# Splitting the row, memory-key and memory-value products of a decoder block into high and low parts, and spreading eight softmax steps over the stream

## The reference

```python
def hybrid_mixer(xn, ...):
    proj = xn @ w_mix_in                     # 1304 columns of q, keys, values, gates; 3 x 512 of the conv
    q, kc, vc, ks, vs, kw, vw, gl, ch, cb, cc = jnp.split(proj, splits, axis=-1)
    q, kc, ks, kw = (rope(a, positions) for a in (q, kc, ks, kw))
    o_nsa = nsa_attention(...)               # compressed keys, and two causal softmaxes, 8 heads in 2 groups
    u = cc * ch                              # conv: 3 taps along the tokens, then times cb
    o = concatenate([rmsnorm(o_nsa), rmsnorm(o_conv)])
    return o @ w_mix_out

h = h + hybrid_mixer(rmsnorm(h), ...)
h = h + memory_cross_attention(rmsnorm(h), rmsnorm(mem), w_xq, w_xkv, w_xo)   # k, v = split(memn @ w_xkv)
h = h + moe_ffn(rmsnorm(h), ...)             # router, top 4 of 32 experts, SwiGLU
return rmsnorm(h, g_final)
```

## Time and profile before

| | |
|---|---|
| time, three runs | 1242.11 us median (1241.1, 1242.11, 1246.43) |
| the profiled execution | 1248.39 us, of which the span of instructions is 1246.4 us |
| PE busy | 1147.8 us, 92% of the span |
| DVE, ACT, POOL busy | 288.1, 186.7, 74.8 us |
| HBM read | 443.6 MB, 357 GB/s over the span |
| mean granted PE clock | 0.989 of 2.4 GHz |

### The profile page before, as it was taken

The page is one execution under the profiler, slowest core; times in us unless marked ns, Lnnn a source line. Parts: engine busy times, 40 slices in busy tenths (PEclk is TensorE's granted clock), DMA queues, the critical chain, the costliest instruction groups (busy, mean ns, idle before and its releaser), DMA issues.

```text
span 1246.4 us, 12486 instructions
## 1 busy us (share of the span) xinstructions
PE 1147.8 (92%) x5441; PEld 493.1 (40%) x5442; DVE 288.1 (23%) x584; ACT 186.7 (15%) x358; POOL 74.8 (6%) x48
## 2 busy tenths in 40 slices
PE   7879988999999999999999899899999998999896
PEld 4576656565433333333333333333333333333332
DVE  3474353221421111221111111121211111111111
ACT  3220354133200000100000000010000000000001
POOL 0450043022000000000000000000000000000000
PEclk9989999999999999999999999999999999999998
DMA  8705503367899999999999999999999999999994
GB/s 339 248 3 231 172 1 135 135 226 293 367 427 427 428 427 427 427 428 427 429 427 429 426 427 428 427 427 428 428 426 428 427 427 426 429 428 427 429 427 175
DMA packets 44135, 445.47 MB, mean 357 GB/s; under 512 B 6040, under 2 KB 10224, under 8 KB 19408
## 3 DMA queue, kind: packets, MB, share of 16 engines
q1 hardware_dynamic: 41936, 444.37, 85.7%
q10 hardware_dynamic: 2144, 0.30, 0.1%
HBM read 443.60 MB, written 1.05 MB: 357 GB/s over the span
## 4 chain that ended last, share of the span: by engine, by line
PE 61%; DMA 32%; DVE 3%; ACT 3%; issue 1%; SPq 0%; DVEq 0%
DMA R<-in_w_gate_up 20%; PE ps L1572 18%; PE ps L1581 13%; DMA XMT<-in_w_gate_up 7%; PE ps L1435 4%; PE ps L1170 4%; DMA XM<-in_w_gate_up 3%; PE ps L1601 3%; PE ps L1548 3%; PE ps L1206 3%; PE ps L1270 2%; PE ps L1228 2%; PE ps L1275 2%; PE ps L1370 2%; PE ps L1563 1%; ACT A L728 1%
## 5 line engine op out<-in xcount | busy, mean ns | idle before, releaser
L1572 PE MATMUL ps<-R,convT 128*64 128x512 f32 x1232 | 274.7, 594 | 26.0 <-DMA R<-in_w_gate_up 26.0
L1097 DVE TENSOR_SCALAR A<-ps 128x512 f32<-128x512 f32 x32 | 22.1, 691 | 695.2 <-PE ps L1572 695.2
L1572 PEld LDWEIGHTS ps<-R,convT 128*64 128x64 f32 x1232 | 85.2, 137 | 203.1 <-issue 149.0
L1581 PE MATMUL ps<-R,A 128*64 128x512 f32 x608 | 134.8, 592 | 0.0
L723 ACT ACTIVATE A<-A 128x512 f32<-128x512 f32 x32 | 20.2, 630 | 508.3 <-DVE A L1097 508.3
L1581 PEld LDWEIGHTS ps<-R,A 128*64 128x64 f32 x608 | 42.7, 137 | 78.2 <-issue 76.8
L1601 PE MATMUL ps<-A,convT 64*128 64x512 f32 x256 | 63.6, 615 | 1.4 <-ACT A L730 1.4
L1548 PE MATMUL ps<-H,convT 128*64 128x512 f32 x256 | 60.4, 592 | 0.3 <-DVE convT L1052 0.3
L730 ACT COPY A<-ps 128x512 f32<-128x512 f32 x32 | 18.7, 585 | 238.4 <-PE ps L1581 238.4
L1572 PE MATMUL ps<-XMT,convT 128*64 128x512 f32 x208 | 47.0, 594 | 3.7 <-DMA XMT<-in_w_gate_up 3.7
L1572 PE MATMUL ps<-QK,convT 128*64 128x512 f32 x208 | 47.0, 594 | 2.4 <-DMA QK<-in_w_gate_up 2.3
(11 more groups left out here) (278 smaller groups left out, 1111.2 us busy)
## 6 DMA issues: line engine op xcount, KB each, us to landing
R<-in_w_gate_up SPq DMA_DIRECT2D x77, 2048.0 KB, 40.9
R<-in_w_down SPq DMA_DIRECT2D x38, 2048.0 KB, 43.3
QK<-in_w_gate_up SPq DMA_DIRECT2D x13, 2048.0 KB, 40.8
A<-in_w_gate_up SPq DMA_DIRECT2D x13, 2048.0 KB, 40.8
XMT<-in_w_gate_up SPq DMA_DIRECT2D x13, 2048.0 KB, 42.2
XM<-in_w_gate_up SPq DMA_DIRECT2D x12, 2048.0 KB, 42.4
XM<-in_w_down SPq DMA_DIRECT2D x7, 2048.0 KB, 44.7
QK<-in_w_down SPq DMA_DIRECT2D x7, 2048.0 KB, 43.3
```

The lines of the kernel that those rows point to most:

```text
L1572: last = mm(bank(b)[s * SLOTS:(s + 1) * SLOTS, :], xg[:, 4 * (j % 2) + 2 * c + j // 2, :], w[:, c * 2 * FF + at + s * BANK:c * 2 * FF + at ...
L1581: last = mm(bank(O_BANK)[s * SLOTS:(s + 1) * SLOTS, :], hTm[:, c, i * SLOTS:(i + 1) * SLOTS], w[:, c * D + s * BANK:c * D + (s + 1) * BANK ...
```

## The change

**Products.** A *unit* is one 512-column block of a weight matrix for one chunk of 128 inputs, split into a high and a low part and multiplied with both halves of the tokens: six matmuls of 512 columns (`unit(u)`, `split_mm`). There are 24 units for the conv (h, c, b, now with tokens on the partitions), 16 for the memory values and 16 for the keys. The rows use the same product (`rows(kc)`, both halves in one pass, three buffers `row_hi`, low parts on DVE). ACT writes every high part; DVE the low parts of rows and conv, POOL those of the memory units. High parts have four buffers up to unit 24 and eight (`HIB`) after.

**Norms.** x and memory are transposed as they come; the root goes in later, as a scale on the way out of PSUM (and in the sine and cosine for the rope). Since the conv and keys now come out with tokens on the partitions, u, b and the keys are transposed after (16 for the conv, 16 for the keys, `key_transposes`).

**Order.** The rope's pieces alternate with the low parts of units 4 to 19 on DVE. The 32 memory units are laid over the softmax steps by `U_AT`, ACT and POOL running `U_AHEAD` = 5 units ahead. On DVE weigh(n) comes right after mask_max(n), and its last instruction is now four `tensor_scalar` in place of one `tensor_tensor`. The hidden layer of the compressed keys uses four column groups of PE in place of two. POOL's constants for the experts wait for the second pv of the cross-attention (it was the second scores), since memory values stand where they are written.

```diff
+HIB = 8
+        ROW_AT = [(R, R_p, kc * ROWC) for kc in range(6)] + [(R, R_p, 22528), (A, A_p, ROWB * ROWC)]
+        row_hi = [QK_p[:, b * ROWC:(b + 1) * ROWC] for b in range(ROWB)]
+        def high(u):
+            i = u % 4 if u < UNITS_X else u % HIB
+            return (R_p[:, 8192 + i * BANK:8192 + (i + 1) * BANK] if i < 4
+                    else XMT_p[:, (i - 4) * BANK:(i - 3) * BANK])
+        def slot_free(u):
+            return u - 3 if u < UNITS_X + 4 else max(u - HIB + 1, UNITS_X)
-        MIX_AT = {1: ["conv", ("w", 4)], 2: [("w", 5)], 3: [("w", 6)], 4: [("w", 7)], 5: [("o", 0), ("w", 0)],
-                  6: [("w", 1), ("w", 2)], 7: [("w", 3)]}
-        KV_AT = {0: [(3, 1), (4, 0)], 1: [(4, 1)], 2: [(5, 0)], 3: [(5, 1)], 4: [(6, 0)], 5: [(6, 1), (7, 0)], 6: [(7, 1)]}
+        MIX_AT = {4: [4, 5], 5: [6, 7], 6: [2, 3], 7: [0, 1]}
+        U_FIRST = 2
+        U_AT = {0: 6, 1: 3, 2: 5, 3: 4, 4: 4, 5: 4, 6: 4}
+        U_AHEAD = 5
+        KV_AFTER = {0: 0, 2: 2, 4: 4, 6: 6}
...
+            # GpSimd
+                def unit_low(u):
+                    pool.wait_ge(act_uhi, u + 1)
+                    nc.gpsimd.tensor_tensor(low(u), raw(u), high(u), ALU.subtract).then_inc(pool_ulo, 1)
...
+            # ScalarE
+                def unit_high(u):
...
+                    if u >= 4:
+                        act.wait_ge(pe_unit, slot_free(u))
+                    nc.scalar.copy(high(u), raw(u)).then_inc(act_uhi, 1)
...
+                for n in range(T * J):
+                    exps(n)
+                    if n == 3:
+                        cmp_exp()
+                    if n >= 1:
+                        pt_out(n - 1)
...
+                    for i_u in range(U_AT.get(n, 0)):
+                        if n == 1 and i_u == 1:
+                            hidden_exp()
+                        if u < UNITS:
+                            unit_high(u)
+                        u += 1
...
+                    if n in KV_AFTER:
+                        kv_out(KV_AFTER[n])
+                        kv_out(KV_AFTER[n] + 1)
+                    for _ in MIX_AT.get(n, []):
+                        weight_high(i)
+                        i += 1
...
             # VectorE, weigh(n)
-                    link(V.tensor_tensor(pb, pb, cof[:, b, :].unsqueeze(2).to_broadcast([P, 4, nk]), ALU.mult), dve_p)
+                    for g in range(G):
+                        for k in range(2):
+                            V.tensor_scalar(Pb[:, b, g, k, 0:nk], Pb[:, b, g, k, 0:nk], cof[:, b, 2 * g + k:2 * g + k + 1], None,
+                                            ALU.mult).then_inc(dve_p, 1)
...
+            # TensorE
+                def split_mm(o, hi, lo, whi, wlo, kc):
+                    mm(o, hi, whi, start=(kc == 0), stop=False)
+                    mm(o, lo, whi, start=False, stop=False)
+                    return mm(o, hi, wlo, start=False, stop=(kc == KC - 1))
...
+                    if q < 3:
+                        pe.wait_ge(dve_ulo, u + 1)
+                    else:
+                        pe.wait_ge(pool_ulo, u - UNITS_X + 1)
+                    for t in range(T):
+                        tok = slice(t * P, (t + 1) * P)
+                        last = split_mm(bank(UNIT_BANKS[q][t]), hi[:, kc, tok], lo[:, kc, tok], high(u), low(u), kc)
+                    last.then_inc(pe_unit, 1)
...
+                    if n == 7:
+                        key_transposes()
...
+                        mix_out(0, 1).then_inc(pe_mo, 1)
                     if n + 1 < T * J:
                         scores(n + 1)
...
                     p_transposes(n)
```

More of the change, by code:

```diff
@@ L37 @@
 SPARE = 3
+HIB = 8
+ROWB = 3
 EPS = 1e-5
@@ L625, in mix_high, with hidden_out @@
[L625 to L633 removed]
+                def hidden_out():
+                    act.wait_ge(pe_hid, 1)
+                    nc.scalar.copy(hid, bank(3)[:, 0:CHID]).then_inc(act_hid, 1)
@@ L1197, in _ @@
[L1197 to L1208 removed]
+                        pe.wait_ge(ld_x[t], 16)
@@ L1220, in conv @@
-                def conv(i):
-                    if i >= 2:
-                        pe.wait_ge(dve_cnv, i - 1)
-                    for which, (b, half) in enumerate(((0, 0), (1, 0), (0, 1))):
-                        pe.wait_ge(pool_lo, 3 * i + which + 1)
-                        hi, lo = w_hi[i][which], w_conv(w_lo, i, which)
-                        for kc in range(KC):
-                            for part, (w, xp) in enumerate(((hi, x_hi), (hi, x_lo), (lo, x_hi))):
-                                last = mm(bank(2 * (i % 2) + b)[:, half * S:(half + 1) * S], w[:, kc, :], xp[:, kc, :],
-                                          start=(kc == 0 and part == 0), stop=(kc == KC - 1 and part == 2))
-                    last.then_inc(pe_cnv, 1)
@@ L1232, in _ @@
-                for i in range(CC - 1):
-                    conv(i)
-                pe.wait_ge(dve_rope, 2)
-                pe.wait_ge(act_rows, 6)
+                x_transposes(3)
+                for kc in range(2, 6):
+                    rows(kc)
+                pe.wait_ge(ld_prm, 16 * 13)
+                tr(bank(7)[:, 0:R_END], prm_rows[:])
+                xg_gain = xg_rows.rearrange("j (n c) -> j c n", c=2)
+                for c in range(2):
+                    last = tr(bank(7)[:, R_XG:R_XG + KC].rearrange("p (a c s) -> p c s a", a=2, c=2)[:, c], xg_gain[:, c, :])
@@ new lines, in _ @@
+                for u in range(2 * KC, 2 * KC + 2):
+                    unit(u)
+                pe.wait_ge(ld_mem, 32)
+                pe.wait_ge(dve_rope, 3)
+                mem_transposes(0)
+                mem_transposes(1)
+                unit(2 * KC + 2)
+                pe.wait_ge(dve_u, 2)
+                for i in range(CC):
+                    for t in range(T):
+                        last = tr(bank(3 + 4 * (i // 2))[:, (i % 2) * S + t * P:(i % 2) * S + (t + 1) * P], u_sb[:, t, i * P:(i + 1) * P])
+                    if i % 2 == 1:
+                        last.then_inc(pe_ubT, 1)
@@ L1326, in scores @@
+                cmp_transposes(4, vrow)
                 def scores(n):
@@ new lines, in hidden @@
+                def hidden():
+                    pe.wait_ge(ld_c1, 32)
+                    pe.wait_ge(dve_blk, 16)
+                    pe.wait_ge(act_kv, 2)
+                    for m in range(8):
+                        for h in range(2):
+                            for v in range(2):
+                                q = 64 * h + 32 * v
+                                last = mm(bank(3)[q:q + 32, 0:CHID], blk[:, v, 8 * h + m], w_c1[:, v, 8 * h + m, :],
+                                          start=(m == 0), stop=(m == 7), skip_group_check=True)
+                    last.then_inc(pe_hid, 1)
@@ new lines, in _, with units @@
+                UNIT_WAIT = {UNITS_V: 4, UNITS_V + KC: 6}
+                def units(n):
+                    for u in range(UNITS_X + n[0], UNITS_X + n[1]):
+                        if u in UNIT_WAIT:
+                            pe.wait_ge(act_kv, UNIT_WAIT[u])
+                        if u == UNITS_X + KC:
+                            pe.wait_ge(dve_blk, 8)
+                        unit(u)
+                at = [0, U_FIRST]
+                for n in range(T * J):
+                    at.append(at[-1] + U_AT.get(n, 0))
```

1072 lines of the change are left out of this document (644 added, 428 removed).

## The result

| | before | after |
|---|---|---|
| median | 1244.27 us (1241.1 to 1246.58, 4 runs) | 1223.51 us (1222.43 to 1223.65, 4 runs) |
| the profiled execution | 1248.39 us, span 1246.4 | 1223.65 us, span 1221.9 |
| mixer's end (transposes of h) | 228.61 | 204.26 |
| PE busy, idle in the mixer | 199.8, 29.0 | 182.5, 21.9 |

The ratio is 0.9833, with a 95% interval of 0.9805 to 0.9861: faster by 1.7%, 20.8 us between the medians. The forecast of 1213 was 10.5 too low; 1223.5 lies in the range of 1194 to 1234, and half a microsecond above the narrower 1204 to 1223 that belonged to waits of 12 to 31 us. The mixer's end is given here by the timeline's row of the eight transposes of h. It begins 0.16 before the chain's in both kernels, since a timeline counts the start of a group and the chain its own step.

The account below looks back on a forecast made before the run. PE bounds the mixer, DMA the experts, which move with the mixer's end. Less work and all old idle time bring 50.4 us, new waits cost 21, so 29.4 off the median 1242.1 gives 1213, range 1194 to 1234.

Parts of the forecast that it names:

- The frame: Whole kernel: the change is worth what it moves the mixer's end at 228.77, one for one; cross-attention and experts keep their length.
- taken back: Rival: the mixer ends early but the experts' weights do not stream earlier, so the time stays 1242; chance 0.04.
- near the floor: Rival: only 6 us of new waits in the mixer, 44 less, 1198; chance 0.15.
- The case with the lock in some steps only: The forecast itself: DVE and POOL shut each other out in some softmax steps, waits 12 to 31, 1213; chance 0.55.
- what feeds the units: Conv and memory units: low parts stay hidden, DVE's 1.3 us against PE's 1.38, POOL's 41 us under PE's 44.2 plus the softmax rest.
- new waits: Mixer: waits the change adds for PE, from start to key transposes, sum 21 us with 3 for lower clock, bounds 6 and 40.
- step 3, two softmaxes on DVE: Softmax step 3: compressed weights wait because DVE does two softmaxes in one step, 2 us.
- step 5, the lock: Softmax step 5: five DVE instructions against POOL's 2.3 us subtractions, each shutting the other out, 5.5 us of wait.
- PE work: Mixer: matmul work removed less added, 25.6 us, plus 3 for work at low clock, so PE needs 171.2 instead of 199.8.
- from the profiled execution to the median: End of the sum: 29.4 less gives 1219.0 from the profile; taken off the median 1242.1, 6.3 lower, it gives 1213.
- Lock throughout: Rival: DVE's five instructions wait for POOL in every softmax step, 39 to 40 us of waits, 10 less, 1232; chance 0.20.
- Slower by queues in order: Rival: in softmax, ACT's ordered queue runs units and chain one after the other, 93 us of waits, 1285; chance 0.06.

## Why the forecast was right, and what was off in it

**The frame held.** The time moved with the mixer's end: from there to the end of the span it is 1016.4 to 1019.5 us in all ten changed kernels (1017.8 before); "taken back" is refuted (91.8 and 925.8 us behind it), and so is "near the floor". The case with the lock in some steps only was the right one.

**Step "what feeds the units": right.** No unit waits for POOL, conv units have no gap.

**Step "new waits": right in kind, too high in sum.** Forecast 7.2 of start and 21 of waits, of which 3 for the clock; measured 21.9 idle.

| | forecast | measured |
|---|---|---|
| start to the first row product | 7.2 + 2 | 9.1 |
| ACT's issues before unit 0 | 3 | none |
| step 0, weigh behind POOL | 2.5 | 2.43 |
| step 1 | 1 | none |
| step 3, two softmaxes on DVE | 2 | 3.19 |
| step 5, the lock | 5.5 | 4.24, and 0.71 for the key copies |
| step 7, key copies | 2 | 2.20 |

That step 5's wait comes in the main from the lock is shown by two edits from opposite sides: fewer multiplies (2.9 off the wait), and POOL's work elsewhere with the multiplies kept (the wait gone, 5.1 us by the multiplies and 1.4 by ACT). For step 0 only the first edit speaks. Step 3's wait had a cause that the forecast did not name: the lock stretches the compressed keys' chain as well. The rows are from the kernel with one multiply, where POOL subtracts from 124 us on:

```profile
124.16 2.33 DVE L1111 SCALAR_TENSOR_TENSOR csm<-csm,valid,gates 128x8 f32<-128x8 f32 x2
126.53 1.43 DVE L1112 TENSOR_TENSOR R<-R,csm 128x240 f32<-128x240 f32 x1
```

In the kernel before, the last of them took 0.41 with POOL silent. No run takes this part away by itself: with two products POOL was done 0.5 us into them (0.80 and 0.41 us), and PE still waited 2.88. How much of the 3.19 is the lock stays open.

One reading of the forecast rests on the wrong row. That the mask instruction, which reads PSUM, stays at 1.23 beside POOL is not shown by the row at 167.04, since POOL had ended at 163.2. It is true all the same: the kernel after took 1.21 for it at 158.23, with POOL subtracting from 158.12 on.

**Step "PE work": this sum was too low, by 11.3 us** (171.2 forecast, 182.5 measured). The unit prices were right: a unit takes 1.38, rows(7) 3.57 from 40.07 to 43.64. What was left out are small kinds of work that changed form and that I did not price, and a low clock in four places. Rows of the kernel after for them:

```profile
16.47 0.29 PE L1427 MATMUL ps<-QK_p,XM_p 128*128 128x280 f32 x1
99.30 3.66 PE L1592 MATMUL ps<-A,R 128*32 128x256 f32 x64
144.77 1.84 PE L1566 MATMUL ps<-ones,QK 128*128 128x1 f32 x16
196.97 1.84 PE L1566 MATMUL ps<-ones,QK 128*128 128x1 f32 x16
```

The sums of squares are 32 records, 1.84 us for each sixteen, where the kernel before had eight in 0.95: 2.7 more. The transposes of the compressed weights are 32 records now, 2.46 us in the runs with four buffers and two products, where sixteen took 1.9: 0.6 more. The hidden layer with four column groups took 3.66, 0.3 less than the 4.0 put in. Work of another form thus makes 3.0. The clock makes the larger part. Those 32 records took 3.86 here (row at 128.99 above), 1.4 more; the first row chunk took 5.7 from 11.58 to 17.24 instead of 3.55, 2.1 more; behind step 5's wait eight transposes (1.97 for 0.89) and six unit matmuls (0.43 for 0.23) took about 2.3 more; and the output product behind the key copies about 1.4 more, by the same rows in the run with fillers. That is 7.2, against the 3 that stood among the waits: this term was sized too low by more than half. Together these make 10.2 of the 11.3; the rest I have not placed.

**Step "from the profiled execution to the median": wrong, by some 5.7 us.** By its own profile the forecast was 1219.0 and the kernel after took 1223.65 in its, 4.7 off: the 11.3 of work less the 6.3 by which idle time was put too high, 28.2 for 21.9 (3 of the 28.2 were the clock's). But I took the 29.4 off the median too, though that profile lay 6.3 above it. Its surplus was not spread over the execution; most of it was the 5 us longer conv wait and the slow matmuls behind it, a part of the time that the change removes. Who starts from 1241.22 and its 222.93 gets 222.9 - 199.4 = 23.5 less and 1217.7. The three times, 1241.1, 1242.1 and 1246.4 with the profile at 1248.4, gave a hint; where the surplus lay only a second profile could tell.

**The rivals.** Lock throughout was refuted: weigh's multiplies were stretched in three steps of eight, one of them hidden, and not in steps 4 and 6, where the forecast had POOL still at work when weigh comes. The time, 1223.5, lies in the middle between the forecast and this rival's 1232, so it is the rows and not the time that part them. Slower by queues in order did not come. Without the cover the kernel takes 1287; that this is near the 1285 of that rival is chance, since it is another program, with other terms.

## What to carry to other kernels

Where a pause of one engine is filled with another's work, count both: taking the filler away costs more than its chain (61 us of waits for 42, and 14 of slower matmuls), and making the filler cheaper pays only in part (4.9 of 14.7 in the profile, 0.6 between the medians). A wait costs more than its length where the matmuls behind it run slowly: of the 5.8 us that the single multiply brought, 4.1 were such matmuls. Where DVE and GpSimd both work on SBUF, use few large DVE instructions, and keep the long GpSimd ones out of the one step whose result PE is waiting for. Before a forecast is moved from a profile to a median, find out where the profile's surplus over the median lies.
